# Expert tiles of 64 rows in a hybrid encoder's mixture of experts, two 64-column matmuls side by side

## The chip, the cores and the metric

The program runs on one NeuronCore of a Trainium2 chip. The metric is device microseconds of an execution, as the median over the runs. One more execution was recorded by the hardware profiler, and all rows below come from that one.

## The reference

Two layers act on 1024 tokens of 1024 channels. In each, one input projection feeds four token mixers (attention with a forget gate, chunked retention, a gated linear recurrence, and attention to 256 memory tokens); their outputs are projected, gated and summed, projected once more, added to the scaled input, and normalised. The change is in the second half of a layer, the grouped mixture of experts:

```python
    probs = jax.nn.softmax((xt @ w_router + b_router).astype(jnp.float32), axis=-1)
    grouped = probs.reshape(T, N_GROUPS, EXPERTS_PER_GROUP)      # T = 1024, 4 groups of 4
    g_sel = jnp.argmax(jnp.max(grouped, axis=-1), axis=-1)
    ...                                                          # top 2 of the chosen group
    flat_e = expert.reshape(-1)
    order = jnp.argsort(flat_e)
    tok = order // TOP_K
    xs = xt[tok]                                                 # 2048 rows of 1024
    h = lax.ragged_dot(xs, w_e_in, group_sizes)                  # 16 experts, 1024 x 1024
    h_gate, h_up = jnp.split(h, 2, axis=-1)
    y = lax.ragged_dot(jax.nn.silu(h_gate) * h_up, w_e_out, group_sizes)   # 512 x 1024
    y = y * weight.reshape(-1)[order][:, None].astype(y.dtype)
    out = jnp.zeros_like(xt).at[tok].add(y.astype(xt.dtype))
```

The 2048 pairs of token and expert are sorted by expert; each expert has between 103 and 163 rows in layer 1 and between 106 and 158 in layer 2.

## The kernel before

A float32 product is computed from float16 parts: each operand is split into a high part (ScalarE, a scaled copy) and a low part (VectorE, `low_part`, line 1016), and TensorE adds high x high, high x low and low x high. `Fori` runs over the two layers; within one, the mixers come first, then the output projection with the router, then the routing, then the expert stage, then the second normalisation.

*Routing* (VectorE lines 1384 to 1488, TensorE lines 1976 to 1991). Ranks of the rows inside their experts come from matmuls with 0/1 matrices. Every expert gets as many tiles of P = 128 rows as it needs (`thr` holds the thresholds). `PICK` (one column for each of TILES = 32 possible tiles) and `PLACE` (one for each row of a tile) are 0/1 tables; their product is `src_row`, which token sits in which row of which tile, and then `row_wt`, the row's weight. A small table `tab` tells each engine the number of tiles, the expert of each tile, and how many experts were loaded up to it (`loads`).

*Expert stage.* One tile i goes through these steps:

1. POOL gathers its 128 rows from `x1_rows` in DRAM by an indirect DMA (`gather_tile`, DMA at line 585).
2. TensorE turns them (`transpose_rows`, eight float32 transposes, line 1570, into `PC`); ScalarE and VectorE make `ROWS` (`row_high`, `row_low`).
3. `first_product` (line 2013): 8 chunks x 3 part products x 2 halves of the columns = 48 matmuls of 128 stationary columns and 512 moving ones, into the two banks of `PA` (gate and up).
4. ScalarE takes `silu` of the gate, VectorE multiplies (`hidden`), TensorE turns the result (`transpose_hidden`, line 2021, four transposes), and both engines split it (`HIDS`).
5. `second_product` (line 2032): 4 x 3 x 2 = 24 matmuls into `PB`.
6. ScalarE scales each row by its weight (`store_rows`, line 920) into `YROW`, and POOL adds the rows into `y_sum` in DRAM by an indirect DMA with accumulation (`add_rows`, line 602). There is one `YROW`, so the store of a tile waits for the landing of the tile before.

TensorE's order in the loop is first product of i + 1, row transposes of i + 2, second product of i, hidden transposes of i + 1. Weights: the SP queue loads an expert's input weights as eight chunks of 512 KB into `WEI`, its output weights as four chunks into `WEO` (`load_ei`, `load_eo`, lines 517 and 523); a chunk is loaded when VectorE has made the low part of the one before it in that place. ScalarE (`ei_high` line 894, `eo_high` line 900) and VectorE (`ei_low`, `eo_low`) split the chunks into `EIS` and `EOS`, each of which holds one expert; a chunk there is overwritten when TensorE has used it for the last tile of its expert (`wei_used`, `weo_used`). All engines walk their steps in a fixed order; `If` skips the weight steps where the next tile has the same expert.

Two places outside the stage are read below because they use matmuls with 64 stationary columns, two heads on different output partitions: `times_v_mem` (line 1733) and, beside it for comparison, `running_sums` (line 1873) with full-width ones.

## Time and profile before

| | us |
|---|---|
| three runs | 3063.25, 3074.59 (median), 3077.78 |
| profiled execution | 3063.31 |
| its span | 3061.6 |
| TensorE busy in the span | 2818.0 (92%) |
| VectorE, ScalarE, POOL busy | 1541.6, 1163.3, 307.1 |

The span is the time from the first to the last instruction on the profiled core. Matmuls are pipelined, so their durations overlap: what one costs in a row of them is the distance from start to start. TensorE's granted clock, 0.956 in the mean, is a share of 2.4 GHz; 0.5 is its lower level, 1.2 GHz. Names such as `XT`, `OT`, `RA`, `W`, `WK`, `BR` in the rows are the buffers that `EIS`, `WEI`, `ROWS` and `WEO`, `EOS`, `HIDS` and `YROW`, and `PICK` and `src_row` lie in. The expert stages lie at 1075 to 1495 us and 2591 to 3008 us.

### The profile page before, as it was taken

The numbers are of one execution on the slowest core, as the hardware profiler recorded it, in microseconds if no ns is written. First come the engines' busy times: TensorE is split into PE (matmuls) and PEld (weight loads), VectorE is DVE, ScalarE is ACT, GpSimd is POOL, SyncE is SP. The second block draws the span as 40 slices with busy tenths as digits, with TensorE's granted clock in tenths as the row PEclk, the third lists the DMA queues.
The fourth block names the chain that finished last, engine by engine and source line by source line (L and its number), as shares of the span: only waits on it lengthen the run. The fifth ranks groups of instructions, "written<-read, shape, count | busy, mean of one in ns | idle before, by whom it ended". The sixth has DMA issues, their size and how long they took to land.

```text
span 3061.6 us, 47346 instructions
## 1 busy us (share of the span) xinstructions
PE 2818.0 (92%) x15748; PEld 1489.9 (49%) x15749; DVE 1541.6 (50%) x2477; ACT 1163.3 (38%) x1845; POOL 307.1 (10%) x240
## 2 busy tenths in 40 slices
PE   6999999999999699999579999999999995999994
PEld 4555554554444445454345555555544453454542
DVE  3244463343345567656633345634433455577665
ACT  3234413222232157655432443222222321576663
POOL 0000000000000023322310000000000000132323
PEclk9999999999999799999779999999999996999996
DMA  7200001111115389977622000111111253699974
GB/s 256 69 1 29 28 19 51 35 39 48 52 63 192 117 289 350 328 253 234 224 96 70 28 1 28 35 35 43 44 52 52 77 189 139 223 340 357 319 253 144
DMA packets 150902, 398.56 MB, mean 130 GB/s; under 512 B 13700, under 2 KB 58928, under 8 KB 149904
## 3 DMA queue, kind: packets, MB, share of 16 engines
q1 hardware_dynamic: 133104, 327.59, 29.4%
q0 software_dynamic: 14816, 54.12, 6.9%
q10 hardware_dynamic: 2816, 14.68, 1.3%
q8 instruction: 99, 1.62, 0.2%
q14 instruction: 67, 0.55, 0.1%
HBM read 343.91 MB, written 56.63 MB: 131 GB/s over the span
## 4 chain that ended last, share of the span: by engine, by line
PE 78%; DVE 6%; issue 5%; PEld 3%; DMA 2%; ACT 2%; DVEq 2%; SPq 0%; POOL 0%; PEldq 0%; ACTq 0%; POOLq 0%
PE PA L2013 15%; PE PA L1589 10%; PE PA L1590 10%; PE PA L1591 10%; PE PB L2032 8%; PE PC L1570 3%; PE PB L1591 3%; PE PB L1589 3%; PE PB L1590 3%; PE PD L1589 1%; PE PD L1591 1%; PE PD L1590 1%; PE PA L1687 1%; PEld PA L1589 1%; PEld PA L1591 1%
## 5 line engine op out<-in xcount | busy, mean ns | idle before, releaser
L2013 PE MATMUL PA<-XT,RA 128*128 128x512 f16 x2304 | 511.2, 382 | 9.7 <-DVE RA L1016 6.2
L1589 PE MATMUL PA<-XT,W 128*128 128x512 f16 x1216 | 461.9, 380 | 0.7 <-issue 0.7
L1590 PE MATMUL PA<-XT,W 128*128 128x512 f16 x1216 | 461.5, 380 | 0.0
L1591 PE MATMUL PA<-XT,W 128*128 128x512 f16 x1216 | 461.4, 379 | 0.0
L2013 PEld LDWEIGHTS PA<-XT,RA 128*128 128x128 f16 x2304 | 226.2, 98 | 277.3 <-issue 15.6
L1016 DVE SCALAR_TENSOR_TENSOR XT<-OT,XT 128x1024 f16<-128x1024 f32 x256 | 295.0, 1219 | 40.6 <-ACT XT L894 40.5
L1016 DVE SCALAR_TENSOR_TENSOR W<-W 128x512 f16<-128x512 f32 (+2 forms) x320 | 199.6, 661 | 163.5 <-ACT W L669 152.2
L819 ACT ACTIVATE WK<-PA,bT 128x512 f32<-128x512 f32 x128 | 87.9, 687 | 496.1 <-PE PA L1591 495.6
L2032 PE MATMUL PB<-W,WK 128*128 128x512 f16 x1152 | 260.8, 384 | 6.7 <-DVE W L1016 4.4
L894 ACT ACTIVATE XT<-OT 128x1024 f16<-128x1024 f32 x240 | 230.9, 1043 | 44.4 <-issue 40.9
L1243 DVE SCALAR_TENSOR_TENSOR MKV<-WK,PB 128x512 f32<-128x512 f32 x96 | 66.0, 687 | 338.9 <-PE PB L1591 338.9
L669 ACT ACTIVATE W<-W 128x512 f16<-128x512 f32 (+2 forms) x320 | 180.9, 601 | 138.5 <-DVE W L1016 86.3
L1591 PEld LDWEIGHTS PA<-XT,W 128*128 128x128 f16 x1216 | 119.0, 98 | 143.9 <-issue 0.8
L1589 PEld LDWEIGHTS PA<-XT,W 128*128 128x128 f16 x1216 | 120.5, 99 | 139.4 <-issue 2.2
L1590 PEld LDWEIGHTS PA<-XT,W 128*128 128x128 f16 x1216 | 119.0, 98 | 135.4 <-issue 0.5
L2032 PEld LDWEIGHTS PB<-W,WK 128*128 128x128 f16 x1152 | 113.6, 99 | 135.7 <-issue 8.2
L582 POOL TENSOR_TENSOR st<-st,CO 128x4 f32<-128x4 f32 x16 | 16.2, 1012 | 1382.7 <-DVE st L1293 1382.7
L1016 DVE SCALAR_TENSOR_TENSOR W<-RA,W 128x1024 f16<-128x1024 f32 x128 | 148.3, 1219 | 5.3 <-ACT W L900 5.3
L1589 PE MATMUL PA<-W,XT 128*128 128x512 f16 (+1 forms) x384 | 132.4, 345 | 1.4 <-issue 1.4
L602 POOL DMA_INDIRECT y_sum<-WK,BR x48 | 129.1, 2689 | 40.5 <-POOL BR L599 37.8
L1591 PE MATMUL PA<-W,XT 128*128 128x512 f16 (+1 forms) x384 | 132.2, 344 | 0.0
L1590 PE MATMUL PA<-W,XT 128*128 128x512 f16 (+1 forms) x384 | 132.2, 344 | 0.0
(348 smaller groups left out, 4229.7 us busy)
## 6 DMA issues: line engine op xcount, KB each, us to landing
OT<-in_w_e_in_dram SPq DMA_DIRECT2D x256, 512.0 KB, 7.6
RA<-in_w_e_out_dram SPq DMA_DIRECT2D x128, 512.0 KB, 8.3
W<-in_w_in_dram SPq DMA_DIRECT2D x104, 512.0 KB, 4.6
W<-in_w_branch_dram SPq DMA_DIRECT2D x32, 256.0 KB, 4.8
W<-in_w_out_dram SPq DMA_DIRECT2D x16, 512.0 KB, 5.2
x_rows<-RC SPq DMA_DIRECT2D x16, 512.0 KB, 5.1
y_sum<-RC SPq DMA_DIRECT2D x16, 512.0 KB, 5.8
OT<-y_sum SPq DMA_DIRECT2D x16, 512.0 KB, 4.3
```

Source lines behind the costliest of these rows:

```text
L602: nc.gpsimd.indirect_dma_start(y_sum, bass.IndirectOffsetOnAxis(at_row[:, 1:2], 0), YROW, None, compute_op=ALU.add).then_inc(y_st, 16)
L669: nc.scalar.activation(WS[slot][:, k, 0, 0:n], W[slot][:, k + SPARE, 0:n], ACT.Copy, scale=SW).then_inc(w_hi, 1)
L819: nc.scalar.activation(TH[g % 2], PA[:, g % 2, :], ACT.Tanh, bias=bT[:, 6 + n * KD + d:7 + n * KD + d], scale=0.5 * UN).then_inc(g_sig, 1)
L894: nc.scalar.activation(EIS[:, 0, k, :], WEI[:, k, :], ACT.Copy, scale=SW).then_inc(ei_hi, 1)
L1016: return stt(dst, src, scale, high, ALU.mult, ALU.subtract)
L1243: stt(acc if place == 0 else ups, TH[g % 2], 1.0, up, ALU.add, ALU.mult).then_inc(g_mul, 1)
L1570: q = nc.tensor.transpose(flat(dst)[:, k * P:(k + 1) * P], src[:, k * P:(k + 1) * P], ident)
L1589: mm(dst, lhs(0), rhs(0), start=first, stop=False)
L1590: mm(dst, lhs(0), rhs(1), start=False, stop=False)
L1591: return mm(dst, lhs(1), rhs(0), start=False, stop=last)
L2013: q = mm(PA[:, half, :], ROWS[:, a, k * P:(k + 1) * P], EIS[:, b, k, half * HALF:(half + 1) * HALF], start=k == 0 and a + b == 0, stop=k = ...
L2032: q = mm(PB[:, half, :], HIDS[:, a, k * P:(k + 1) * P], EOS[:, b, k, half * HALF:(half + 1) * HALF], start=k == 0 and a + b == 0, stop=k = ...
```

## The change

A tile now has HT = 64 rows, and TILES grows to 52 (in PAIRS = 26). Rows are still gathered and turned 128 at a time, for a pair of half tiles (`gather_pair`, `transpose_rows(j)`), but each half has its own expert. In `first_product` and `second_product` the 64 rows of a half are the stationary columns; two matmuls with the same stationary rows write output partitions 0 to 63 and 64 to 127, each for one half of the output's columns. In `first_product` that is half of the gate's columns and half of the up columns (256 of either), so one bank of `PA` holds a half tile, with `silu` and `hidden` over 256 elements and two hidden transposes. `PA`, `PB`, `PD`, `SIL`, `HID`, `HIDS` and `YROW` exist twice, for even and odd halves. The second product of a half follows two first products later instead of one. The store is two instructions of 64 x 512 elements; rows are scattered per half, each scatter issued when the one before has landed. SP loads an expert's input and output weights in one go. The routing's tables grow with TILES. VectorE's order follows ScalarE's.

```diff
-TILES = 2 * T // P + E
+HT = P // 2
+TILES = 2 * T // HT + E + 4
+PAIRS = TILES // 2
+HF = FE // 2
+THR = T // HT
...
-        YROW = WK[:, 2048:3072]
-        src_row = BR[:, NT * P:NT * P + TILES].bitcast(U32)
-        row_wt = BR[:, NT * P + TILES:NT * P + 2 * TILES]
-        at_row = BR[:, NT * P + 2 * TILES:NT * P + 2 * TILES + 2].bitcast(U32)
-        PICK = BR[:, 0:NT * P].bitcast(F16).rearrange("p (a s) -> p a s", a=2 * NT)
+        YROW = [WK[0:HT, 2048 + i * D:2048 + (i + 1) * D] for i in range(2)]
+        SIL = [WK[:, i * HF:(i + 1) * HF] for i in range(2)]
+        HID = [WK[:, FE + i * HF:FE + (i + 1) * HF] for i in range(2)]
...
-        HIDS = WK[:, 1024:1536].bitcast(F16).rearrange("p (s n) -> p s n", s=2)
+        HIDS = [WK[:, 1024 + i * HF:1024 + (i + 1) * HF].bitcast(F16).rearrange("p (s n) -> p s n", s=2) for i in range(2)]
...
-                with sp.If(loads(sp, 0) < loads(sp, 1)):
-                    load_ei(1, e0 + 1)
-                with sp.Fori(1, last) as i:
-
-                    c0, c1, c2 = loads(sp, i - 1), loads(sp, i), loads(sp, i + 1)
-                    with sp.If(c1 < c2):
-                        load_ei(i + 1, c1)
+                with sp.Fori(0, last * 2 + 1) as h:
+
+                    c0, c1 = loads(sp, h), loads(sp, h + 1)
                     with sp.If(c0 < c1):
-                        load_eo(i, c0)
-                c0, c1 = loads(sp, before_last), loads(sp, last)
-                with sp.If(c0 < c1):
-                    load_eo(last, c0)
+                        load_expert(h + 1, c0)
...
+                def gather_pair(j):
+
+                    pool.wait_ge(row_tr, g0 + j)
+                    pool.sem_inc(passed, 1)
+                    nc.gpsimd.tensor_copy(at_row[:, 0:1], pair_row[:, bass.ds(j, 1)]).then_inc(at_src, 1)
+                    pool.wait_ge(at_src, g0 + j + 1)
                     pool.sem_inc(passed, 1)
                     gather(at_row[:, 0:1])
 
-                def add_rows(i):
-
-                    pool.wait_ge(y_ev, g0 + i + 2)
-                    nc.gpsimd.tensor_copy(at_row[:, 1:2], src_row[:, bass.ds(i, 1)]).then_inc(at_dst, 1)
-                    pool.wait_ge(at_dst, g0 + i + 1)
+                def add_rows(p, o, b):
+                    h = p * 2 + o
+                    pool.wait_ge(y_ev, (g0 + p) * 2 + (o + 5))
                     pool.sem_inc(passed, 1)
-                    nc.gpsimd.indirect_dma_start(y_sum, bass.IndirectOffsetOnAxis(at_row[:, 1:2], 0), YROW, None,
+                    nc.gpsimd.tensor_copy(at_row[0:HT, 1 + b:2 + b], src_row[0:HT, bass.ds(h, 1)]).then_inc(at_dst, 1)
+                    pool.wait_ge(y_st, (g0 + p) * 32 + (o + 1) * 16)
+                    pool.wait_ge(at_dst, (g0 + p) * 2 + (o + 1))
+                    pool.sem_inc(passed, 1)
+                    nc.gpsimd.indirect_dma_start(y_sum, bass.IndirectOffsetOnAxis(at_row[0:HT, 1 + b:2 + b], 0), YROW[b], None,
                                                  compute_op=ALU.add).then_inc(y_st, 16)
...
+                with pool.Fori(1, before_last) as j:
+                    gather_pair(j + 2)
+                    add_rows(j, -1, 1)
+                    add_rows(j, 0, 0)
+                for j in (before_last, last):
+                    add_rows(j, -1, 1)
+                    add_rows(j, 0, 0)
...
-
-                    act.wait_ge(row_tr, g0 + i + (l + 1))
-                    nc.scalar.activation(ROWS[:, 0, :], flat(PC), ACT.Copy, scale=SX).then_inc(row_hi, 1)
...
+                def row_high(j, b):
+
+                    if b == 0:
+                        act.wait_ge(row_tr, g0 + j + 1)
+                    else:
+                        act.wait_ge(row_lo, (g0 + j) * 2 + 1)
+                    nc.scalar.activation(ROWP[:, 0, :, b, :], turned_rows[:, :, b, :], ACT.Copy, scale=SX).then_inc(row_hi, 1)
+
...
+                def store_rows(p, o, b, after=True):
+                    h = p * 2 + o
+                    act.wait_ge(weo_used, (g0 + p) * 2 * KF + (o + 4) * KF)
 
                     if after:
-                        act.wait_ge(y_st, (g0 + i) * 16)
-                    nc.scalar.activation(YROW, flat(PB), ACT.Copy, scale=row_wt[:, bass.ds(i, 1)]).then_inc(y_ev, 1)
-
-                def act_step(i):
-
-                    c0, c1, c2 = loads(act, i - 1), loads(act, i), loads(act, i + 1)
-                    with act.If(c1 < c2):
-                        ei_high(i + 1, c1)
-                    store_rows(i - 1)
-                    hidden_high(i)
+                        act.wait_ge(y_st, (g0 + p) * 32 + o * 16)
+                    for i in range(2):
+                        rows = slice(i * HT, (i + 1) * HT)
+                        q = nc.scalar.activation(YROW[b][:, i * HALF:(i + 1) * HALF], PB[rows, b, :], ACT.Copy,
+                                                 scale=row_wt[rows, bass.ds(h, 1)])
+                    q.then_inc(y_ev, 1)
+
...
+                with act.Fori(0, near + 1) as i:
+                    j = i + 2
+                    silu(j, -1, 1)
+                    next_out(j, -2)
+                    row_high(j, 1)
+                    store_rows(i, 1, 1)
+                    next_expert(j * 2)
+                    hidden_high(j, -1, 1)
+
+                    silu(j, 0, 0)
+                    next_out(j, -1)
+                    row_high(j + 1, 0)
+                    store_rows(i + 1, 0, 0)
+                    next_expert(j * 2 + 1)
+                    hidden_high(j, 0, 0)
...
                 tt(PICK[:, :, 3 * TILES:4 * TILES], over(tile_f, TILES),
                    co("iota128")[:, 0:TILES].unsqueeze(1).to_broadcast([P, 2 * NT, TILES]), ALU.is_equal)
...
+                for b in range(2):
+                    rows = slice(b * HT, (b + 1) * HT)
+                    q = ts(pair_row[rows, :], PC[rows, 0, 0:TILES].rearrange("p (j b) -> p b j", b=2)[:, b, :],
+                           co("rowid")[rows, :], 2.0 * T, ALU.add, ALU.add)
+                q.then_inc(inv_ok, 1)
...
+                ts(small[:, 256:256 + PAIRS], co("iota128")[:, 0:PAIRS], 2.0, cum[:, E - 1:E], ALU.mult, ALU.is_lt)
+                v.drain()
+                nc.vector.tensor_reduce(tabf[:, TILES:TILES + 1], small[:, 256:256 + PAIRS], AX.X, ALU.add)
...
+                with v.Fori(2, last) as j:
+                    hidden(j, -1, 1)
+                    next_out(j * 2 - 2)
+                    row_low(j, 1)
+                    next_expert(j * 2)
+                    hidden_low(j, -1, 1)
+
+                    hidden(j, 0, 0)
+                    next_out(j * 2 - 1)
+                    row_low(j + 1, 0)
+                    next_expert(j * 2 + 1)
+                    hidden_low(j, 0, 0)
...
-                def first_product(i, c):
-                    pe.wait_ge(row_lo, g0 + i + (l + 1))
+                def first_product(h, b, c):
+                    pe.wait_ge(row_lo, g0 * 2 + h + 1)
                     for k in range(KD):
                         pe.wait_ge(ei_lo, c * KD + (k + 1))
-                        for a, b in ((0, 0), (0, 1), (1, 0)):
-                            for half in range(2):
-                                q = mm(PA[:, half, :], ROWS[:, a, k * P:(k + 1) * P],
-                                       EIS[:, b, k, half * HALF:(half + 1) * HALF],
-                                       start=k == 0 and a + b == 0, stop=k == KD - 1 and a == 1)
+                        for a, w in ((0, 0), (0, 1), (1, 0)):
+                            for i in range(2):
+                                q = mm(PA[i * HT:(i + 1) * HT, b, :].rearrange("p (g n) -> p g n", g=2),
+                                       ROWP[:, a, k, b, :],
+                                       EIS[:, w, k, :].rearrange("p (g i n) -> p i g n", g=2, i=2)[:, i, :, :],
+                                       start=k == 0 and a + w == 0, stop=k == KD - 1 and a == 1)
                         q.then_inc(wei_used, 1)
...
+                def transpose_hidden(p, o, b):
+                    pe.wait_ge(hid_ok, (g0 + p) * 2 + (o + 1))
+                    for k in range(2):
+                        q = nc.tensor.transpose(PD[:, b, k * P:(k + 1) * P], HID[b][:, k * P:(k + 1) * P], ident)
...
+                def second_product(p, o, b, c):
+                    pe.wait_ge(hid_lo, (g0 + p) * 2 + (o + 3))
...
+                        for a, w in ((0, 0), (0, 1), (1, 0)):
+                            for i in range(2):
+                                q = mm(PB[i * HT:(i + 1) * HT, b, :],
+                                       HIDS[b][:, a, k % 2 * P + k // 2 * HT:k % 2 * P + (k // 2 + 1) * HT],
+                                       EOS[:, w, k, i * HALF:(i + 1) * HALF],
+                                       start=k == 0 and a + w == 0, stop=k == KF - 1 and a == 1)
                         q.then_inc(weo_used, 1)
...
-                with pe.Fori(0, last) as i:
-                    c1, c2 = loads(pe, i), loads(pe, i + 1)
-                    first_product(i + 1, c2)
-                    transpose_rows(i + 2)
-                    second_product(i, c1)
-                    transpose_hidden(i + 1)
-                second_product(last, loads(pe, last))
+                first_product(1, 1, loads(pe, 1))
+                transpose_hidden(0, 0, 0)
+                with pe.Fori(1, last) as j:
+                    c0, c1, c2, c3 = (loads(pe, j * 2 + i) for i in (-2, -1, 0, 1))
+                    first_product(j * 2, 0, c2)
+                    transpose_hidden(j, -1, 1)
+                    second_product(j, -2, 0, c0)
+
+                    transpose_rows(j + 1)
+                    first_product(j * 2 + 1, 1, c3)
+                    transpose_hidden(j, 0, 0)
+                    second_product(j, -1, 1, c1)
```

## Rows read from the trace of the kernel before

**Rows 1.** Busy us by engine, granted clock, DMA share, GB/s: the two expert stages.

```profile
1075.00:1495.00 420.00, 410.71 (x2016) 203.11 (x2016) 271.38 (x257) 248.27 (x277) 114.73 (x92) 0.98 0.83 283
...
2591.00:3008.00 417.00, 410.43 (x2016) 202.64 (x2016) 271.35 (x257) 248.54 (x277) 117.02 (x91) 0.99 0.82 286
```

**Rows 2.** TensorE's timeline, one tile: start us, us, engine, line, operation, count.

```profile
1111.00 10.52 PE L2013 MATMUL PA<-XT,RA 128*128 128x512 f16 x48
1121.36 1.04 PE L1570 MATMUL PC<-CO,RA 128*128 128x128 f32 x8
1122.24 5.34 PE L2032 MATMUL PB<-W,WK 128*128 128x512 f16 x24
1127.42 0.60 PE L2021 MATMUL PD<-CO,WK 128*128 128x128 f32 x4
1127.85 2.32 PE L2013 MATMUL PA<-XT,RA 128*128 128x512 f16 x10
```

**Rows 3.** Groups by shape, layer 1's stage: busy us, mean ns, idle before.

```profile
L2013 PE MATMUL PA<-XT,RA 128*128 128x512 f16 x1152 | 255.5, 382 | 5.1 <-DVE XT L1016 2.6 <-DVE RA L1016 2.5
...
L2032 PE MATMUL PB<-W,WK 128*128 128x512 f16 x576 | 130.9, 385 | 4.4 <-DVE W L1016 4.4
```

**Rows 4.** TensorE's timeline in layer 1: memory attention, then a gated recurrence's sums.

```profile
183.44 0.38 PE L1591 MATMUL PD<-W,XT 128*128 128x512 f16 x1
183.75 1.09 PE L1733 MATMUL PD<-WK,MKV 128*64 128x128 f32 x16
184.77 0.44 PE L1570 MATMUL PC<-CO,WK 128*128 128x128 f32 x2
...
491.08 1.56 PE L1873 MATMUL PC<-BR,CO 128*128 128x256 f32 x6
492.48 0.50 PE L1875 MATMUL PC<-CO,BR 128*128 128x2 f32 x4
```

**Rows 5.** Timeline of the weight loads in the same stretch.

```profile
183.75 0.85 PEld L1733 LDWEIGHTS PD<-WK,MKV 128*64 128x64 f32 x16 [0.42 <-issue]
```

**Rows 6.** Busy us by engine, granted clock, DMA share of that stretch.

```profile
183.40:185.10 1.70, 1.70 (x21) 1.17 (x20) 0.96 (x4) 0.26 (x1) 0.00 (x0) 1.00 0.00 0
```

**Rows 7.** DMA queues from 1066 to 1495 us: packets, MB, share of 16 engines.

```profile
q1 hardware_dynamic: 25920, 94.38, 58.2%
q0 software_dynamic: 6894, 25.10, 23.1%
```

**Rows 8.** Busy us, clock, DMA share, GB/s of 40 us in layer 1's stage.

```profile
1140.00:1180.00 40.00, 40.00 (x201) 19.97 (x200) 24.31 (x24) 22.56 (x26) 10.89 (x11) 1.00 1.02 349
```

**Rows 9.** TensorE's timeline where it stood still in the two stages.

```profile
1094.14 6.22 PE L2013 MATMUL PA<-XT,RA 128*128 128x512 f16 x28 [2.64 <-DVE XT L1016]
...
2785.40 2.76 PE L2013 MATMUL PA<-XT,RA 128*128 128x512 f16 x12 [0.47 <-DVE XT L1016]
```

**Rows 10.** Groups by shape, layer 1's stage, other engines.

```profile
L1016 DVE SCALAR_TENSOR_TENSOR XT<-OT,XT 128x1024 f16<-128x1024 f32 x120 | 137.6, 1220 | 19.4 <-ACT XT L894 19.4
...
L894 ACT ACTIVATE XT<-OT 128x1024 f16<-128x1024 f32 x120 | 115.3, 1043 | 20.2 <-issue 20.2
...
L920 ACT ACTIVATE WK<-PB,BR 128x1024 f32<-128x1024 f32 x24 | 26.5, 1103 | 67.1 <-DMA y_sum<-WK,BR 47.2 <-PE PB L2032 19.8
...
L909 ACT ACTIVATE WK<-PD 128x512 f16<-128x512 f32 x24 | 14.0, 582 | 0.0
```

**Rows 11.** Groups by shape of the whole span: a 256-element step.

```profile
L1016 DVE SCALAR_TENSOR_TENSOR OT<-ON,OT 128x256 f16<-128x256 f32 x32 | 13.6, 425 | 38.9 <-ACT OT L744 38.9
```

**Rows 12.** The scatter's line: from issue to landing.

```profile
DMA to landing us min/median/max: 5.8/9.6/13.4
```

**Rows 13.** Timeline of all engines at the end of layer 1's stage.

```profile
1494.42 1.11 ACT L920 ACTIVATE WK<-PB,BR 128x1024 f32<-128x1024 f32 x1 [6.83 <-PE PB L2032]
...
1502.62 11.24 SPq L550 DMA_DIRECT2D OT<-y_sum  x7
```

**Rows 14.** Timeline in the routing of layer 1.

```profile
1065.12 0.68 DVE L1461 TENSOR_TENSOR WK<-WK,CO 128x512 f32<-128x512 f32 x1
```

More of the change, by code:

```diff
@@ L884, in _ @@
                 act.sem_inc(passed, 1)
-                before_last = act.value_load(tab[0:1, TILES + 2:TILES + 3], min_val=E - 2, max_val=TILES - 3)
-                last = before_last + 1
-                g0 = act.value_load(tab[0:1, TILES + 1:TILES + 2], min_val=0, max_val=TILES)
-                def ei_high(i, before):
-                    for k in range(KD):
+                near = act.value_load(tab[0:1, TILES + 2:TILES + 3], min_val=E // 2 - 4, max_val=PAIRS - 6)
+                before_last = near + 2
@@ L891, in ei_high, with eo_high @@
+                last = near + 3
+                g0 = act.value_load(tab[0:1, TILES + 1:TILES + 2], min_val=0, max_val=PAIRS)
+                def ei_high(h, before, chunks):
+                    for k in chunks:
                         act.wait_ge(wei_ld[k], (before + 1) * 16)
-                        act.wait_ge(wei_used, (g0 + i) * KD + (k + 1))
+                        act.wait_ge(wei_used, (g0 * 2 + h) * KD + (k + 1))
                         nc.scalar.activation(EIS[:, 0, k, :], WEI[:, k, :], ACT.Copy, scale=SW).then_inc(ei_hi, 1)
-                def eo_high(i, before):
+                def eo_high(p, o, before):
@@ new lines, in _ @@
+                silu(last, -1, 1)
+                next_out(last, -2)
+                row_high(last, 1)
+                store_rows(near + 1, 1, 1)
+                next_expert(last * 2)
+                hidden_high(last, -1, 1)
+                silu(last, 0, 0)
+                next_out(last, -1)
+                store_rows(near + 2, 0, 0)
+                hidden_high(last, 0, 0)
+                silu(last, 1, 1)
+                next_out(last, 0)
+                store_rows(near + 2, 1, 1)
+                hidden_high(last, 1, 1)
@@ new lines, in hidden_low, with hidden, next_expert @@
+                def hidden_low(p, o, b):
+                    v.wait_ge(hid_hi, (g0 + p) * 2 + (o + 1))
+                    low_part(HIDS[b][:, 1, :], PD[:, b, 0:HF], SX, HIDS[b][:, 0, :]).then_inc(hid_lo, 1)
+                def hidden(p, o, b):
+                    v.wait_ge(hid_sil, (g0 + p) * 2 + (o + 1))
+                    stt(HID[b], PA[:, b, HF:FE], UN, SIL[b], ALU.mult, ALU.mult).then_inc(hid_ok, 1)
+                def next_expert(h):
+                    c0, c1 = loads(v, h), loads(v, h + 1)
+                    with v.If(c0 < c1):
+                        ei_low(c0, range(KD))
@@ L1530, in _, with next_out @@
+                def next_out(h):
+                    c0, c1 = loads(v, h - 1), loads(v, h)
                     with v.If(c0 < c1):
                         eo_low(c0)
-                    hidden(i + 1)
-                    row_low(i + 2)
-                hidden_low(last)
-                c0, c1 = loads(v, before_last), loads(v, last)
-                with v.If(c0 < c1):
-                    eo_low(c0)
+                row_low(0, 0)
+                eo_low(e0)
+                next_expert(0)
+                row_low(0, 1)
@@ L1540, in _ @@
+                hidden(last, -1, 1)
+                next_out(last * 2 - 2)
+                row_low(last, 1)
+                next_expert(last * 2)
+                hidden_low(last, -1, 1)
+                hidden(last, 0, 0)
+                next_out(last * 2 - 1)
+                hidden_low(last, 0, 0)
+                hidden(last, 1, 1)
+                next_out(last * 2)
+                hidden_low(last, 1, 1)
+                next_out(last * 2 + 1)
                 for t in range(NT + 3):
@@ L2101, in constants @@
     put("ones", np.ones((P, 16)))
-    put("thr", np.tile(np.where(np.arange(8) == 0, -1, np.arange(8) * P), (P, 1)))
+    put("thr", np.tile(np.where(np.arange(THR) == 0, -1, np.arange(THR) * HT), (P, 1)))
+    put("rowid", i % HT - T)
     put("iota128", np.tile(i, (P, 1)))
```

250 lines of the change are left out of this document (120 added, 130 removed).

## The prediction

> **What bounds the kernel now.** I read the busy shares of the two expert stages first, then TensorE's timeline inside one tile, then the groups by shape, then the DMA queues, and last the few places where TensorE stood still. In both expert stages TensorE is busy for 411 of 420 us and 410 of 417 us at a granted clock of 0.98 to 0.99, that is its 2.4 GHz level; VectorE has 271 us of work in a stage, ScalarE 248, and the DMA engines are busy 0.83 of it [rows 1]. One tile reads as first product 10.36 us (start to start), row transposes 0.88, second product 5.18, hidden transposes 0.43, and the next tile starts without a gap: 16.85 us a tile [rows 2]. So a half of the kernel that the change doesn't touch stays as it is, and an expert stage costs its tiles on TensorE: 1152 and 576 matmuls, 48 and 24 a tile, make 24 tiles [rows 3], and 24 x 16.85 = 404 us.
>
> How full the tiles are follows from the reference's inputs. Counting rows per expert gives, in 128-row tiles, 1 1 1 2 1 1 2 1 2 2 2 2 2 1 2 1 in layer 1 and 2 2 1 2 1 1 1 1 2 1 1 2 2 1 2 2 in layer 2, 24 in each. In 64-row halves each "1" becomes 2 and each "2" becomes 3: 40 in each layer, 20 pairs without padding.
>
> **The change, part by part.**
> *The products.* A half tile issues as many matmuls as a tile did (48 + 24), each with 64 stationary columns and 512 moving ones, the two of a pair on different output partitions. Everything hangs on whether a pair runs side by side. The attention shows it in float32: 16 instructions of 128*64 by 128 columns take 1.02 us to the next start, 64 ns each [rows 4], at a granted clock of 1.00 [rows 6]. Full-width float32 instructions take 0.88 / 8 = 110 ns for 128 columns as transposes [rows 2], and as products (492.48 - 491.08) / 6 = 0.23 us for 256 columns [rows 4]. Two narrow ones at a time, then, at 55 ns each, plus 0.15 us. For float16 I take the same: a pair costs one 512-column stream, 10.36 / 48 = 216 ns. First product 24 x 0.216 = 5.18, second 12 x 0.216 = 2.59: 7.77 us a half.
> *Transposes.* Eight row transposes for a pair of halves, 0.44 a half; two hidden ones of 0.11, 0.22 a half.
> *Changing between widths.* The 128*64 stretch starts 0.31 us after the last full-width matmul, whose own step is 0.22: 0.09 us on the way in. On the way out 1.02 - 16 x 0.055 = 0.15 us [rows 4]. A round trip costs 0.24 us. In the loop of a pair the order is first product, hidden transposes, second product, row transposes, first, hidden transposes, second: three round trips, 0.36 us a half. A half is thus 7.77 + 0.44 + 0.22 + 0.36 = 8.79 us, 40 of them 352 us, and a stage is 404 - 352 = 52 us shorter if nothing else is late.
>
> The Trainium skill, "TensorEngine Tiling (Array Packing)", section Key Properties, says that changing the tiling mode drains TensorE. By that rule the round trips cost; the rows above put 0.24 us on each, so 3 x 20 x 2 x 0.24 = 29 us in the sum. Without the rule the sum would be 29 us lower.
>
> *DMA.* In the 429 us of layer 1's stage the weight queue moves 94.38 MB in 58.2% of the engines' time, 250 us, and the gathers and scatters take 23.1%, 99 us, for 24 tiles [rows 7]. An expert's weights are then 250 / 15 = 16.6 us; a tile's gather and scatter 4.1. Bytes of rows go down by 20 / 24 in the gathers and 40 x 64 / (24 x 128) = 0.83 in the scatters: 2.07 us a half. An expert of two halves has 17.6 us of TensorE and 16.6 + 4.1 = 20.7 us of DMA; one of three has 26.4 and 22.8. Even now the engines are full for 40 us at a time (1.02) [rows 8], and after the run of four one-tile experts in layer 2 TensorE waits 0.47 us for a chunk [rows 9]. Only one expert is loaded ahead, and SP now issues an expert's input and output weights together, so that the next input weights are queued behind a wait for the output buffer (behind that wait stand eight loads, and for those wait ScalarE's and VectorE's splits and then TensorE). I charge 1.5 us each time that two experts of two halves follow one another (3 times in layer 1, 4 in layer 2), and 1 us more for the start: 6 us a stage; ends 0 and 14 (the 3.1 us by which DMA is longer at four or five of the eight two-half experts).
>
> *Splitting the weights.* Eight input chunks and four output chunks an expert, 115.3 / 120 = 0.96 us on ScalarE and 137.6 / 120 = 1.15 on VectorE each in a run of them [rows 10], unchanged in number. Row, hidden and product steps now come per half: 512 columns 0.58 on ScalarE [rows 10] and about 0.7 on VectorE (the 0.68 of [rows 14]), 256 columns 0.43 [rows 11]. The store becomes two instructions of 64 x 512, some 0.6 us each where one of 1.10 was [rows 10]. Per stage VectorE has 15 x 12 x 1.15 + 40 x (0.69 + 2 x 0.43) = 269 us, ScalarE 15 x 12 x 0.96 + 40 x (0.6 + 2 x 0.43 + 1.2) = 279 us, both under 352. They collide at experts of three halves: the output chunks of the expert and the input chunks of the next fall into one half's time. Counted from the start of that half's first product, ScalarE begins the output chunks at -2.4 (as the second product before frees them), is through at 1.8, has row step and store behind it at 3.6 and the first input chunk at 4.6; VectorE ends the last at 4.6 + 8 x 1.15 = 13.8. TensorE wants that one at the half's end plus 7 x 6 x 0.108 = 4.5, that is at 12.9 without row transposes between and 13.8 with them. 0 to 0.9 us, eight times: 3 us a stage; ends 0 and 10.
>
> *Scatters.* POOL now waits until a scatter has landed before it issues the next, and 40 of them must fit. Behind its wait stand the next gather and scatter, behind them ScalarE's store, which holds up the splits. A 128-row scatter lands after 5.8 / 9.6 / 13.4 us (least, median, most) [rows 12]; in layer 1's stage ScalarE already waits 47 us for them [rows 10]. For 64 rows no row stands. Bounds: a fixed part alone and half the rows, 3 us, to no gain at all, 9.6. I take 7, nearer to the rows under load, below 8.79: 3 us a stage for the slow ones.
>
> *Routing.* Tables of 52 tiles instead of 32: a 512-element step of 0.68 us [rows 14] grows by 320 elements, 0.33 us (1.22 - 0.68 us over 512 elements [rows 10, 14]). Ten such steps stand on the path to the table, with three small new ones: 4.5 us a layer. Ends 2 and 7.
>
> *Start and end.* At the start the second expert's products wait 2.64 us for split weights [rows 9]; two products at the lower clock lie before them then, and I take this wait as gone, 3 us. At the end 8.2 us pass from the last store's start to the first load of sums [rows 13]; now two scatters stand one behind the other there, 2 us more.
>
> *Sum.* A layer: 52 - 6 - 3 - 3 - 4.5 - 2 + 3 = 37 us (36.5), both 73. Profiled execution 3063.3 (its span 3061.6 and 1.7 around it) - 73 = 2990. The median of the runs shown is 11 us above that execution, whose time is their lowest; I leave the forecast at 2990. With every uncertain term at its good end 2 x (52 + 3 - 2 - 2) = 102: 2961; with free width changes 2932. With all at the bad end 2 x (52 - 14 - 10 - 6 - 7 - 4) = 22: 3041.
>
> **Rivals.**
> A. *DMA becomes the bound.* If the software queue's cost goes by instruction and not by row, 60 gathers and scatters instead of 48 take 99 x 60 / 48 = 124 us; with 250 that is 374, plus some 22 us for the last expert's products: 396 us against 404 + some 10 now for start and end. A gain of 18 a layer less 4.5 of routing: 3036. For it: 1.02 busy in a stretch [rows 8]. Against: bytes fall, and the mean is 0.83 [rows 1].
> B. *The scatters' chain, slower than before.* One landing per half; if 64 rows take L, a stage takes 40 x (L + 0.2). It decides from 8.6 us and turns into a loss at (404 - 6) / 40 - 0.2 = 9.8. At 11.5, between median and most [rows 12], 468 us: 64 + 6 more a layer, 3203. For it: landings under full DMA. Against: half the bytes, and no weights load through half the stage. At 9.6 it gives 392 us, and with 6 of routing and end 3052.
> C. *Pairs don't run side by side in float16.* 40 x (2 x 7.77 + 1.02) = 662 us, 258 + 4.5 more a layer: 3588. Against it the 64 ns of rows 4.
> D. *Weight loads stand between the pairs.* A load of 64 columns is stepped at (0.85 - 0.14) / 15 = 48 ns [rows 5]; two exposed for each of 36 x 80 pairs are 276 us: 3266. Against: those 16 loads cost no time beside their matmuls.
>
> The Trainium skill, "TensorE: Matmul & The Clock Gate", section The mechanism, says that a weight load overlaps matmuls in flight only where its row group differs, which here it never does. That is rival D. The trace disagrees at full width too: 98 ns of load are hidden in each 216 ns step.
>
> **How the numbers follow.** Forecast 0.71; A 0.12; B 0.10 (half of it beyond the turning point); C 0.02; D 0.02; width changes free, under 2940, 0.03. Range 2938 to 3060: above it lie B's worse part, C and D, 0.10 or so, and below it 0.03 and a little of the forecast's edge; A is inside. What a measurement can't tell from no change is 0.5%, from 3059 to 3090 around the median of the runs: inside lies a part of B and the edge of A, 0.06. Slower: the rest of B, C and D, 0.09. Faster 0.85.
>
> **What would show it.** Products: 48 narrow matmuls in about 5.2 us, 24 in 2.6, and 40 such halves a layer; 10.4 is C, near 7.5 D. Width changes: 0.09 us before and 0.15 after a narrow stretch. DMA: share 0.9 and more over the stage, and TensorE's idle time named for input chunks in the two-half experts; A would show a share of 1.0 throughout and a longer sum of the software queue. Scatters: the landing for 64 rows near 7 us; ScalarE's store waiting for the sums in most halves would be B. Routing: TensorE's idle time before the first gathered rows longer by 4 to 5 us. The prediction is wrong if a half takes more than 9.9 us on average, or less than 8.5.

## The result, and the profile after

The changed kernel takes 3111.5 us (median of 4 runs, 3110.0 to 3117.9), the kernel before 3069.0 in the runs beside them (3063.3 to 3077.8): 1.014 times as long, 95% interval 1.0106 to 1.0174. The forecast was 2990 and faster. It was wrong by 121 us and in its sign.

The products became as short as forecast. TensorE's timeline of one unstalled pair of half tiles (start us, us, engine, line, operation, count, idle before):

```profile
1189.92 5.37 PE L2105 MATMUL PA<-XT,RA 128*64 128x512 f16 x48 [1.28 <-issue]
1195.22 0.44 PE L2114 MATMUL PD<-CO,WK 128*128 128x128 f32 x2
1195.59 2.78 PE L2125 MATMUL PB<-W,WK 128*64 128x512 f16 x24
1198.30 1.09 PE L1661 MATMUL PC<-CO,RA 128*128 128x128 f32 x8
1199.32 5.37 PE L2105 MATMUL PA<-XT,RA 128*64 128x512 f16 x48
```

48 narrow matmuls step in 5.30 us and 24 in 2.71, two at a time; a half is 9.40 us with the row transposes and 8.28 without, 17.7 a pair (forecast 17.6). The second figure is from pairs where the next first product follows without a gap. But the first row already shows 1.28 us in which TensorE waited for nothing that the profile names ("issue"). No such gap stands at the head of a tile in [rows 2]. The two stages (busy us of TensorE, weight loads, VectorE, ScalarE, POOL; granted clock, DMA share, GB/s):

```profile
1083.40:1506.40 423.00, 375.10 (x3112) 184.03 (x3112) 267.18 (x303) 275.97 (x378) 103.66 (x114) 0.96 0.80 270
2612.40:3051.00 438.60, 377.55 (x3112) 183.12 (x3112) 268.76 (x303) 278.08 (x378) 103.71 (x114) 0.97 0.76 260
```

They answer to [rows 1]: TensorE's work fell from 411 to some 376 us, the stages grew from 418.3 and 415.5 to 423.0 and 438.6 us, TensorE is idle for 48 and 61 us in them, the clock fell from 0.98 and 0.99 to 0.96 and 0.97, and the DMA engines are less busy than before, not more. The span is 49.7 us longer: 4.6 and 23.1 in the stages, 3.7 in each routing, 4.8 and 5.6 behind the last product of each stage, and 3.8 in layer 1's mixers, whose code is the same. Those 3.8 us mean little: layer 1's stage begins at 1075.9, 1080.4 and 1084.6 us in `before`, `before_loads` and `before_joint` (experiments 6 and 3), three kernels with the same work on TensorE up to there.

The worst stretch is the row of two-half experts in layer 2 (TensorE, then SP's issues of weights there):

```profile
2740.53 0.44 PE L2114 MATMUL PD<-CO,WK 128*128 128x128 f32 x2
2741.18 0.84 PE L2125 MATMUL PB<-W,WK 128*64 128x512 f16 x6 [0.22 <-DVE W L1060]
...
2748.96 8.24 PE L2105 MATMUL PA<-XT,RA 128*64 128x512 f16 x48 [3.53 <-issue]
...
2764.10 0.84 PE L2105 MATMUL PA<-XT,RA 128*64 128x512 f16 x6 [0.43 <-DVE XT L1060]
```

```profile
2741.36 3.68 SPq L531 DMA_DIRECT2D RA<-in_w_e_out_dram  x4
2750.38 6.29 SPq L528 DMA_DIRECT2D OT<-in_w_e_in_dram  x8
2771.52 3.68 SPq L531 DMA_DIRECT2D RA<-in_w_e_out_dram  x4
2780.58 6.11 SPq L528 DMA_DIRECT2D OT<-in_w_e_in_dram  x8
```

The same issues in the kernel before:

```profile
2735.78 3.67 SPq L523 DMA_DIRECT2D RA<-in_w_e_out_dram  x4
2743.06 8.06 SPq L517 DMA_DIRECT2D OT<-in_w_e_in_dram  x8
2752.60 3.66 SPq L523 DMA_DIRECT2D RA<-in_w_e_out_dram  x4
2759.90 8.07 SPq L517 DMA_DIRECT2D OT<-in_w_e_in_dram  x8
```

In this stretch an expert comes every 16.8 us before and every 30.2 us after. The four output chunks are issued in both as VectorE's splits free their buffers; the eight input chunks follow. Whether they were ready long before is told by SP's waits (us, times, longest us), in layer 1's stage before, then after:

```profile
SPq L517 <- DVE XT L1016: 107.8, 80, 21.1
SPq L523 <- DVE W L1016: 91.1, 44, 11.6
```

```profile
SPq L531 <- DVE W L1060: 188.4, 53, 19.6
SPq L528 <- DVE XT L1060: 7.8, 12, 1.4
```

Before, SP waits for each input chunk's buffer (L517), so it issues it as soon as it is free. After, it hardly waits for one (L528, 7.8 us): they had been free, and SP stood in front of them at an output buffer (L531, 188 us). ScalarE then waits for the landing, 72.2 us in the whole kernel (the line is from the page of the profile; before, its waits had 3.5 us for this), at 5 experts of layer 1's stage and 8 of layer 2's:

```profile
L902 ACT ACTIVATE XT<-OT 128x1024 f16<-128x1024 f32 x240 | 238.9, 1048 | 87.8 <-DMA OT<-in_w_e_in_dram 72.2
```

The scatters did little. Their line shows who waited for them (us, times):

```profile
  POOL y_sum L606: 96.9, 33
  ACT WK L934: 6.4, 2
```

POOL waits, ScalarE's store hardly ever (6.4 us, where it was 80.8 in the kernel before); only at a stage's end do they stand on the path:

```profile
1503.64 1.42 POOL L606 DMA_INDIRECT y_sum<-WK,BR  x1 [0.77 <-POOL BR L602]
...
1509.14 1.43 POOL L606 DMA_INDIRECT y_sum<-WK,BR  x1 [3.38 <-DMA y_sum<-WK,BR]
...
1514.78 1.42 POOL L606 DMA_INDIRECT y_sum<-WK,BR  x1 [4.01 <-DMA y_sum<-WK,BR]
1519.57 1.76 SPq L551 DMA_DIRECT2D OT<-y_sum  x4
```

Three 64-row scatters stand one behind the other, 5.5 us apart, where [rows 13] had one.

### The profile page after: what moved, and what is told of

Read it like the earlier page. It is cut to its first block, busy times and chain, and to the rows that moved or that the text cites. A ratio compares the mean times of both kernels' runs of the same rounds, so it can differ in the third digit from the quotient of the medians.

```text
span 3111.3 us, 54474 instructions
## 1 busy us (share of the span) xinstructions
PE 2750.4 (88%) x17940; PEld 1451.0 (47%) x17941; DVE 1545.3 (50%) x2577; ACT 1221.1 (39%) x2051; POOL 284.6 (9%) x286
## 4 chain that ended last, share of the span: by engine, by line
PE 59%; issue 10%; DMA 9%; DVE 7%; ACT 4%; PEld 3%; SPq 3%; DVEq 3%; ACTq 1%; POOL 0%; PEldq 0%; POOLq 0%
PE PA L1680 10%; PE PA L1681 10%; PE PA L1682 10%; DMA OT<-in_w_e_in_dram 5%; PE PA L2105 5%; PE PB L1682 3%; PE PB L1680 3%; PE PB L1681 3%; PE PC L1661 2%; DMA y_sum<-WK,BR 1%; PE PD L1680 1%; ACT XT L902 1%; PE PD L1682 1%; SPq L528 1%; PE PD L1681 1%
## 5 line engine op out<-in xcount | busy, mean ns | idle before, releaser
L2105 PE MATMUL PA<-XT,RA 128*64 128x512 f16 x3840 | 464.6, 397 | 96.3 <-DVE XT L1060 47.9
L2105 PEld LDWEIGHTS PA<-XT,RA 128*64 128x64 f16 x3840 | 218.7, 114 | 328.7 <-issue 90.4
L902 ACT ACTIVATE XT<-OT 128x1024 f16<-128x1024 f32 x240 | 238.9, 1048 | 87.8 <-DMA OT<-in_w_e_in_dram 72.2
L2125 PE MATMUL PB<-W,WK 128*64 128x512 f16 x1920 | 227.3, 382 | 15.1 <-DVE W L1060 15.1
L2125 PEld LDWEIGHTS PB<-W,WK 128*64 128x64 f16 x1920 | 99.7, 109 | 118.9 <-DVE W L1060 30.7
```

The costliest lines, as they stand in the source:

```text
L902: nc.scalar.activation(EIS[:, 0, k, :], WEI[:, k, :], ACT.Copy, scale=SW).then_inc(ei_hi, 1)
L2105: q = mm(PA[i * HT:(i + 1) * HT, b, :].rearrange("p (g n) -> p g n", g=2), ROWP[:, a, k, b, :], EIS[:, w, k, :].rearrange("p (g i n) -> p ...
L2125: q = mm(PB[i * HT:(i + 1) * HT, b, :], HIDS[b][:, a, k % 2 * P + k // 2 * HT:k % 2 * P + (k // 2 + 1) * HT], EOS[:, w, k, i * HALF:(i + 1 ...
```

## The experiments

Times are medians of 4 to 10 runs, ratios are to the kernel before, with 95% intervals.

**1. SP's order** (`sp_order`).

```
     with sp.Fori(...) as h:
         c0, c1 = loads(sp, h), loads(sp, h + 1)
         with sp.If(c0 < c1):
-            load_expert(h + 1, c0)
+            load_ei(h + 1, c0)
+        d0, d1 = loads(sp, h - 3), loads(sp, h - 2)
+        with sp.If(d0 < d1):
+            load_eo(h - 2, d0)
```

> SP issues an expert's input weights at its own transition and its output weights three halves later, so that the input weights of the next expert no longer stand behind the wait for the output buffer. Theory 1 (the order of SP's issues made the chunks late): both stages get shorter by 20 to 40 us together or more, about 3060 in all; ScalarE's wait for input chunks (72 us in the changed kernel) falls under 20. Theory 2 (TensorE's sequencer: register loads and the branch exposed once a pair): nothing but what the chunks gave, the 1.2 to 1.7 us gaps ahead of the even halves stay. Theory 3 (DMA capacity): no change, 3111, since the bytes are the same.

Measured: 3044.6 us, ratio 0.991 (0.987 to 0.994). 67 us less than the changed kernel, and faster than before. Theory 1 holds. The stages are 399 and 396 us, and the wait for input chunks is back at SP. ScalarE's wait for their landing, 72.2 us, is gone from its list of waits:

```profile
SPq L527 <- DVE XT L1071: 98.5, 75, 12.4
```

The gap at the head of the pairs stayed, at an unhindered pair too:

```profile
1160.25 5.37 PE L2116 MATMUL PA<-XT,RA 128*64 128x512 f16 x48 [1.85 <-issue]
```

**2. SP's loop** (`sp_fixed_new`, `sp_fixed_old`): no loop, a list of the 16 experts.

```
-    with sp.Fori(0, last * 2 + 1) as h:
-        ...
+    load_ei(1)
+    for n in range(2, E): load_ei(n); load_eo(n - 1)       # sp_fixed_new, then load_eo(E - 1)
+    for n in range(1, E): load_ei(n); load_eo(n)           # sp_fixed_old
```

> The same order, but SP's list of experts is written out for these inputs (every expert has rows): no loop over halves, no table reads, no branches on SP. Theory 1 with the cost of SP's loop (about 2.4 us per half with no load): 10 to 30 us below the version with the table, about 3040. If only the order mattered, the same time as with the table. Theory 3: 3111.

> The changed kernel with SP's list of experts written out for these inputs, in its own order (an expert's eight input chunks, then its four output chunks). If the order alone made the chunks late (the new order brought 67 us, and writing the list out in the new order another 7): about 3105. If the loop over halves on SP (some 2.4 us a half from the last issue of one burst to the first of the next) was a good part of it: 3060 to 3080.

Measured: 3038.0 us, ratio 0.990 (0.986 to 0.993), and 3095.7 us, ratio 1.006 (1.004 to 1.009). The loop is worth 16 us in the old order, between the two expectations, and 7 in the new one, where the single runs overlap (3036.4 to 3048.1 without it, 3040.4 to 3050.9 with it). The order is worth 58 without a loop and 67 with it. The order is the cause of most of the lateness, the loop in the old order of a part.

**3. The same order at full-width tiles** (`before_joint`): the kernel before, input and output weights issued together.

```
-    c0, c1, c2 = loads(sp, i - 1), loads(sp, i), loads(sp, i + 1)
-    with sp.If(c1 < c2): load_ei(i + 1, c1)
-    with sp.If(c0 < c1): load_eo(i, c0)
+    c0, c1 = loads(sp, i), loads(sp, i + 1)
+    with sp.If(c0 < c1): load_ei(i + 1, c0); load_eo(i + 1, c0)
```

> The kernel before, with 128-row tiles, but SP issues an expert's input and output weights together, as the changed kernel does, instead of the input weights a tile earlier than the output weights. If the joint issue costs by itself (67 us were had back by undoing it at half tiles): 20 to 60 us more than before, 3095 to 3130. If it costs only where an expert's products on TensorE take about as long as its loads (17.6 us for two half tiles, against 16.85 us for a tile here, so the same holds): the same 20 to 60. If the tiles' 16.85 us and the longer steps cover it: within 10 us of before.

Measured: 3138.1 us, ratio 1.022 (1.020 to 1.024): 65 us more, a little over what was expected. The joint issue costs about the same in a kernel that has no half tiles, and ScalarE's wait for the landing of input chunks comes with it (72.8 us). TensorE at the first product of an expert there:

```profile
1147.35 12.63 PE L2006 MATMUL PA<-XT,RA 128*128 128x512 f16 x48 [9.23 <-DVE XT L1009]
```

The product starts 9.2 us late and then takes 12.6 us for what takes 10.5 in [rows 2].

**4. A quarter of the bytes** (`light_weights` on the changed kernel, `sl_light` on `sc_late` of experiment 7). Both leave out three quarters of the columns of every expert's weights but a layer's first.

```
-    sp.dma_start(WEI[:, k, :], w_e_in[l, e, k * P:(k + 1) * P, :])
+    sp.dma_start(WEI[:, k, 0:256], w_e_in[l, e, k * P:(k + 1) * P, 0:256])     # WEO too
```

> Every load of a weight chunk after the first expert's of a layer moves a quarter of its columns (left out: the other three quarters, the products run on stale numbers there). Order and waits are as in the changed kernel. Theory 3 (capacity or landing time of the DMAs): the stages fall by 100 us together, to about 3010. Theory 1: the chunks are still issued late, but land some 3 us sooner after issue; 20 to 50 us less, 3070 to 3090. Theory 2: 3111 less what chunks gave; the gaps once a pair stay.

> The version with SP's new order and one read at the head of TensorE's round (3029.1 us), with every load after a layer's first expert's moving a quarter of its columns (left out: the other three quarters). If the DMA engines' capacity is what is left (share 0.82 of the stage): 15 to 40 us less, about 3000. If VectorE's splits and the stage's start are what is left, as the halved splits say: under 8 us less.

Measured: 3082.7 us, ratio 1.003 (1.002 to 1.005), 29 us less than the changed kernel; and 3039.5 us, ratio 0.991 (0.988 to 0.993), 10 us more than `sc_late`'s 3029.1. These totals can't be taken as they stand. What is left out changes layer 1's output and so layer 2's routing, and layer 2's stage has 42 half tiles instead of 40. Its first products in `sc_late`, then in `sl_light`:

```profile
L2118 PE MATMUL PA<-XT,RA 128*64 128x512 f16 x1920 | 221.5, 384 | 9.7 <-DVE XT L1071 5.2 <-DVE RA L1071 2.9 <-issue 1.5
L2118 PE MATMUL PA<-XT,RA 128*64 128x512 f16 x2016 | 233.2, 384 | 10.8 <-DVE XT L1071 6.1 <-issue 2.8 <-DVE RA L1071 1.5
```

Layer 1's stage compares like with like: 407.7 us in `light_weights` for 423.0, and 383.6 in `sl_light` for 394.3. Less 17.7 us for the added pair, an estimate, the totals are some 46 us below the changed kernel and some 7 below `sc_late`. With or without the pair the first lies in theory 1's range of 20 to 50: what is issued late lands sooner (median of the output chunks 2.1 us for 3.6). `sl_light` had a DMA share of 0.48 (layer 1's stage):

```profile
1083.30:1466.90 383.60, 365.39 (x3112) 179.31 (x3112) 264.73 (x303) 272.78 (x378) 108.17 (x114) 0.99 0.48 113
```

Capacity isn't the bound in either: if it were, 100 us less were expected in the one and 15 to 40 in the other. Up to 11 us of `sc_late`'s layer 1 stage may still be the DMA's.

**5. What the gap at the head of a pair is.** TensorE's round reads four expert numbers from the table, one for each product. First the round was made twice as long (`pe_unroll`, on the changed kernel):

```
-    with pe.Fori(1, last) as j:
-        c0, c1, c2, c3 = (loads(pe, j * 2 + i) for i in (-2, -1, 0, 1))
+    with pe.Fori(1, last, 2) as j0:
+        c = [loads(pe, j0 * 2 + i) for i in range(-2, 4)]
+        for j in (j0, j0 + 1): ...
```

> TensorE's loop takes two pairs a round: 9 branches and 9 x 6 reads of expert numbers a layer instead of 18 and 18 x 4. Theory 2 (TensorE's register work is exposed): half of the 18 gaps of 1.2 to 1.7 us in each layer vanish and the others are up to half longer for six reads: between -5 and -25 us, about 3095. Theory 1 or 3 alone: nothing, since TensorE then waits for the chunks instead: 3111.

Measured: 3137.4 us, ratio 1.022 (1.019 to 1.025), 26 us more: a miss. Half of the gaps were gone, the others mostly 2.7 to 5.1 us long. That spoke for the fetch of instructions as well as for the reads. In sum the gaps ahead of the even halves are 27 and 29 us in the two stages, less than the 31 and 34 of the changed kernel, so where the 26 us come from stays open. Three versions on that of experiment 1 told them apart:

```
+    with nc.Fori(1, last, engines=only_pe, hint_back_edge=True) as j:       # so_hint
+    c0, c1 = (nc.snap(r) for r in kept)                                     # so_carry
+    c2, c3 = (loads(pe, j * 2 + i) for i in (0, 1))
+    ...
+    nc.regs_mov(kept[0], c2); nc.regs_mov(kept[1], c3)      # at the round's end
+    for i in (-2, -1, 0, 1): loads(pe, j * 2 + i)           # so_loads: once more
```

> On the version with SP's new order (3044.6 us), where TensorE still starts nearly every even half 1.2 to 2.8 us late, 18 times a layer: TensorE's loop announces its closing branch at the top of each round, so that the instructions at the loop's head are fetched ahead. Theory A (the gap is the fetch of instructions after the taken branch; twice the body, twice the gap was seen in the unrolled loop): the gaps fall to under 0.5 us, 18 x 2 x 1.2 = 43 us less, about 3000. Theory B (the gap is the four reads of expert numbers and their register work): no change, 3045.

> On the same version: two of the four expert numbers that TensorE reads a round are kept in registers from the round before, so two reads instead of four. Theory B: the gaps halve, 18 x 2 x 0.7 = 25 us less, about 3020. Theory A: 0 to 3 us less, 3042 to 3045.

> On the same version: four more reads of the table at the top of TensorE's round, their values unused. Theory B: the gaps grow by as much as they are, 18 x 2 x 1.2 to 1.6 = 43 to 58 us more, about 3095. Theory A: under 10 us more, since the reads run while or after the instructions come.

Measured, against 3044.6: the hint 3056.8 us, ratio 0.994 (0.993 to 0.996), 12 more (this loop is also opened in another way, `nc.Fori`, and the two were not told apart); two reads 3030.4 us, 0.986 (0.983 to 0.988), 14 less; eight reads 3179.5 us, 1.036 (1.032 to 1.041), 135 more. The mean gap over the 19 pairs of layer 1's stage was 0.29 us with two reads, 1.64 with four and 3.7 with eight: 0.5 to 0.7 us for each read beyond two. By these means six reads would give some 2.7 us, an estimate; the unrolled loop has 3.0 and 3.3 us a round in the two stages. What is left there may be a fetch; nothing tested it. With eight the cost is more than twice the 43 to 58 us expected; behind a gap the product itself is longer:

```profile
1191.92 7.91 PE L2116 MATMUL PA<-XT,RA 128*64 128x512 f16 x48 [3.79 <-issue]
```

```profile
1180.00:1200.00 20.00, 16.21 (x124) 7.58 (x120) 8.38 (x12) 10.25 (x14) 4.46 (x6) 0.83 0.96 316
```

Behind 3.8 us of standing still the product takes 7.9 us for 5.4, and the granted clock is 0.83 in these 20 us. So theory B holds in its sign and mechanism, though none of its sizes (no change, 25 us less, 43 to 58 more) was met, and the branch's fetch was not shown to cost anything in this loop. The Trainium skill, "Runtime: NRT & Kernel Launch", section Instruction fetch mechanics, says that a taken branch to code outside of the window forces a fetch, an argument for theory A; no run here shows it in this loop. The same section gives some 200 ns a register for the register load TENSOR_LOAD, which by that page reads from HBM; a read here is from a table on the chip and cost, with the register work around it, 0.5 to 0.7 us.

**6. The reads at full width, and under the old order** (`before_loads`: four reads a tile for two; `pe_carry`: two for four on the changed kernel; edits as above).

> The kernel before, with TensorE's reads of expert numbers a round doubled from two to four, 23 rounds a layer. If TensorE's sequencer ran far enough ahead of the 216 ns matmuls to hide its register work (no gap at a round's start is seen there), the time stays: within 5 us of before. If reads are exposed at any width, 23 x 2 x 0.6 = 28 us more.

> The changed kernel (3111.5 us) with SP's order as it is, but two reads of expert numbers a round on TensorE instead of four. If the two causes add up, as on the version with SP's new order (3044.6 to 3030.4): 14 us less, 3097. If the chunks' lateness covers the reads while SP's order is the old one: 0 to 5 us less.

Measured: 3087.9 us, ratio 1.004 (1.003 to 1.006), 14 more than before, 0.3 us a tile, between the two expectations. Two reads are worth 14 us at half tiles too (3044.6 to 3030.4, 0.4 us a round), so the widths don't differ much there; four more at half tiles cost 135 / 36 = 3.7 us a round, which was not tried at full width. And 3103.6 us, ratio 1.010 (1.007 to 1.012): 8 less, near half of the 14 it brings once the chunks are in time, and between the two expectations. The two causes seem to overlap.

**7. What is left** (`sc_late`: the second read stands ahead of the row transposes; `sc_halfsplit`: on `so_carry`, half of each input chunk is split, the other half left out after a layer's first expert; `sc_written`: `sc_late` with the list of experiment 2).

```
-    c2, c3 = (loads(pe, j * 2 + i) for i in (0, 1))
+    c2 = loads(pe, j * 2)                                       # sc_late
+    ...
+    c3 = loads(pe, j * 2 + 1)                                   # ahead of transpose_rows
-    low_part(EIS[:, 1, k, :], WEI[:, k, :], SW, EIS[:, 0, k, :])
+    low_part(EIS[:, 1, k, 0:HALF], WEI[:, k, 0:HALF], SW, EIS[:, 0, k, 0:HALF])   # sc_halfsplit
```

> The version with SP's new order and two reads kept in registers (3030.4 us), with the second of the two reads moved from the head of TensorE's round to before the row transposes, whose 110 ns instructions leave the sequencer time. If 0.6 us a read is exposed only where the queue of matmuls is short: the 0.3 us a round that is left at the head goes, 12 us less, 3018 to 3028. If a read costs as much wherever it stands: no change.

> The same version, where ScalarE and VectorE split only half of the columns of each input chunk (left out: the split of the other 512 columns of input weights after a layer's first expert). Theory: what is left over the 352 us of products is VectorE's rate, 1.13 us a chunk against 0.65 us in which TensorE uses one up, at the experts of three halves: 20 of the 24 us of idle time in each stage go, about 3000. Rival (DMA or the start of the stage bounds): under 10 us less.

> The same version with SP's list of experts written out in the new order for these inputs: no loop on SP. If what the list brought under four reads (7 us) adds up: about 3022. If SP is early enough by now: 3029, no change.

Measured: `sc_late` 3029.1 us, ratio 0.985 (0.984 to 0.987), not told from 3030.4, though the gaps fell to 0.15 us: VectorE's chunks took their place. `sc_halfsplit` 3015.9 us, 0.982 (0.979 to 0.984), 14.5 less than `so_carry`, although it too has the added pair in layer 2's stage (2016 matmuls of first products); without it, by the estimate of experiment 4, it would be 32 less, near the 3000 expected. Layer 1's stage took 370.4 us for 389.9. `sc_written` 3025.7 us, 0.985 (0.983 to 0.988), the fastest that computes everything; its 3 us over `sc_late` are inside the noise. VectorE's pace, in `sc_late`:

```profile
1233.96 0.84 PE L2118 MATMUL PA<-XT,RA 128*64 128x512 f16 x6 [0.30 <-DVE XT L1071]
1235.09 0.84 PE L2118 MATMUL PA<-XT,RA 128*64 128x512 f16 x6 [0.30 <-DVE XT L1071]
1236.23 0.84 PE L2118 MATMUL PA<-XT,RA 128*64 128x512 f16 x6 [0.30 <-DVE XT L1071]
```

A chunk every 1.13 us, where TensorE uses one up in 0.66. With half splits layer 1's stage is 370 us long, and TensorE works 359 of them:

```profile
1084.20:1454.60 370.40, 358.91 (x3112) 183.68 (x3112) 204.69 (x303) 225.63 (x378) 88.73 (x114) 0.99 0.86 309
```

## Why the prediction was wrong, step by step

- **Products, transposes, width changes: right.** 40 halves of 8.79 us were to make 352 us; TensorE's busy time is 359 once nothing disturbs it. Pairs run side by side (rival C is out). By the sign that the prediction set for itself, more than 9.9 us a half, it failed all the same: the stages are 10.6 and 11.0 us a half, since idle time is in them. A narrow load of 109 to 114 ns is hidden behind its 110 ns step; by the rule of the Trainium skill given with rival D ("TensorE: Matmul & The Clock Gate", section The mechanism) it would stand in the open, and the trace disagrees at this width too.
- **DMA, the step that failed.** The prediction saw that "the next input weights are queued behind a wait for the output buffer" and then priced it as capacity: 1.5 us where two two-half experts meet, 6 us a stage, end 14. It is latency, and ScalarE stands waiting for it at 13 of the 30 experts loaded behind the first ones. An output buffer is freed by the split of the expert's output weights, which waits for the last second product of the expert before; the input buffers are free earlier, but were issued behind it. From there to the next expert's first product lie SP's issue, the landing, and the chunks' way through ScalarE and VectorE. Undoing the order brought 67 us where 12 were charged, and doing it to the kernel before cost 65. A count of queues' bytes can't show this; rows 7 and 8 were the wrong rows for it, the waits of SP the right ones. Nor did the DMA share reach the 0.9 that was to show it: it was 0.80 and 0.76.
- **The term that was missing: TensorE's own sequencer.** With two reads a tile of 216 ns matmuls no gap showed at the head of a tile, and the sum put this work at nothing. The change made it four reads a round of narrow matmuls, and these left 31 and 34 us of gaps in the two stages. Keeping two in registers brought 14 us once SP's order was mended, 8 before.
- **Clock.** The sum was made at 0.98 and had no term for what idle time does to it. In the changed kernel first products of 6.9 to 8.2 us for 5.4 stand behind gaps of 2.5 us and more; over the one of 8.24 us, from 2748.9 to 2757.2 us, the granted clock is 0.64.
- **Splits:** 3 us a stage were charged, end 10; halving the split of the input chunks shortened layer 1's stage by 20 us, so this term was too small and its end too. It was worked out for experts of three halves alone.
- **Scatters:** 7 us taken for 64 rows; the median landing was 7.0 in `sc_late`. They cost next to nothing inside the stage, 3 us were charged. Rival B did not happen: the sign was its sign, the mechanism not its mechanism.
- **Routing:** 4.5 taken, 3.7 measured. **Start:** 3 taken; where 2.64 us of waiting stood, 0.87 and 0.30 us are left in layer 1. **End:** 2 taken, 4.8 and 5.6 measured, since three scatters stood in a row, not two.
- **Rival A** (DMA) is out: 0.76 to 0.80 busy in the changed kernel, and a quarter of the bytes brings some 7 us, by the estimate of experiment 4, once the order is mended.

By size: 67 + 14 us for the two causes, then the splits' pace, 20 us in layer 1's stage. From 2999 (the 73 us below the median of before, 3072) to `sc_written` 27 us remain, 37 in the profiled executions. There the stages are 31.0 and 36.8 us shorter, where the sum has 43 each: 18 us short, which the splits' pace can account for. Outside the stages 31.6 us are added, where the sum has 13: the two ends have 4.4 and 9.9 of them for 2 and 2, the two routings some 7 for 9, and the other 10 are about what executions of the same code differ by. That the tail's scatters could be had back was not tried.

## What to carry to other kernels

An issue queue that puts loads with different release times in one burst makes the early one as late as the late one: order the issues by when their buffers come free, and look for the wait that vanishes from the list of waits (L528) as the sign. Before halving an engine's instructions, count what its sequencer does per round, since gaps that two reads did not leave among matmuls of 216 ns came with four among those of 110. And a change that shortens the busiest engine's work can make a chain beside it the bound: price each by its latency, not only its share. When a version leaves out part of the data, check that what depends on the data, here the number of tiles, is still the same before its time is compared.

## What the runs showed that was not expected

- Reads of a table value into TensorE's registers lengthen the gap by 0.5 to 0.7 us each beyond the first two in a round of narrow matmuls. Four more in each of 36 rounds cost 135 us, of which some 80 are gaps; of the rest the longer products after a gap are what the timeline shows.
- Announcing the loop's closing branch cost 12 us instead of bringing any.
- The bytes of the weights matter little once SP's order is right: with a quarter of them layer 1's stage takes 383.6 us, with all of them 394.3. Layer 2's takes 399.2 for 382.6, but with the added pair.
- Indirect scatters of 64 rows land after 4.5 to 10.0 us, median 7.0, in `sc_late`, and at the end of a stage of the changed kernel they stand 5.5 us apart; [rows 12] has 5.8 to 13.4 for 128.
